# Slot loads that wait for the steady count of splits, small tables behind the second weight slot, and two activation sums behind the low parts

## The reference, cut to what matters

```python
def hybrid_layer(x, pos, ckv_past, kr_past, p):
    h = rms_norm(x, p['g_mix'])
    z = h @ p['w_in']                     # 1024 -> 256 q | 128 kv | 32 key | 512 u | 512 v
    ...                                   # latent attention (8 heads) and spatial gating
    x = x + merged @ p['w_o']             # 1024 -> 1024
    h2 = rms_norm(x, p['g_ffn'])
    x = x + (jax.nn.silu(h2 @ p['w_gate']) * (h2 @ p['w_up'])) @ p['w_down']   # 1024 -> 2816 -> 1024
    return x, c_kv, k_r, v_rows
```

## Time and profile before

| | |
|---|---|
| time, median of 3 runs | 1525.26 us (1521.08 to 1540.3) |
| the profiled execution's own time | 1518.49 us |
| its span, first to last instruction | 1516.7 us |
| mean granted TensorE clock | 0.966 |
| PE busy | 1369.4 us (90%) |
| PE weight loads busy | 1259.9 us (83%) |
| DVE busy | 902.1 us (59%) |
| POOL busy | 847.3 us (56%) |
| ACT busy | 577.0 us (38%) |
| HBM read | 98.10 MB, 67 GB/s over the span |

### The profile page before, as it was taken

One profiled execution on the slowest core, in us unless ns is written; L12 is line 12 of the kernel. 1 busy time (PEld: TensorE's weight loads), 2 busy tenths in 40 slices (PEclk: granted clock), 3 DMA queues, 4 the chain that ended last, 5 costly groups with the idle time before them and its releaser, 6 DMA issues.

```text
span 1516.7 us, 25316 instructions
## 1 busy us (share of the span) xinstructions
PE 1369.4 (90%) x9496; PEld 1259.9 (83%) x9496; DVE 902.1 (59%) x1490; ACT 577.0 (38%) x925; POOL 847.3 (56%) x452
## 2 busy tenths in 40 slices
PE   6998978978989898989879989899699898989898
PEld 6885656978989898989778755679699898989898
DVE  3458567256757575756544585762666666656575
ACT  4335566242323333333142354662333333333331
POOL 4535247436767575757264443454476666757571
PEclk9999999989999999999989999999899999999999
DMA  6200011112131313223321000011122223131321
GB/s 214 77 20 9 1 56 57 49 36 84 57 111 55 106 60 101 65 90 104 93 77 56 24 4 29 29 56 56 39 73 75 93 72 94 58 108 56 110 83 63
DMA packets 125967, 102.33 MB, mean 67 GB/s; under 512 B 8652, under 2 KB 112528, under 8 KB 125904
## 3 DMA queue, kind: packets, MB, share of 16 engines
q1 hardware_dynamic: 123240, 100.46, 21.4%
q10 hardware_dynamic: 2664, 1.02, 0.3%
HBM read 98.10 MB, written 3.36 MB: 67 GB/s over the span
## 4 chain that ended last, share of the span: by engine, by line
PE 36%; issue 23%; POOL 22%; DVE 13%; ACT 3%; DMA 2%; SPq 1%; ACTq 0%; POOLq 0%; DVEq 0%
POOL w_lo L865 8%; PE ps L2139 7%; POOL w_lo_a L865 5%; PE ps L1810 3%; PE ps L1814 3%; PE ps L1811 3%; PE ps L1793 3%; PE ps L1795 3%; PE ps L1794 3%; POOL w_lo L875 3%; PE ps L1755 3%; PE ps L2043 2%; DVE hs_lo L1246 2%; POOL gate L852 2%; PE ps L2023 2%
## 5 line engine op out<-in xcount | busy, mean ns | idle before, releaser
L735 POOL TENSOR_TENSOR rs<-ms,mhalf 128x8 f32<-128x8 f32 (+5 forms) x66 | 140.5, 2133 | 219.6 <-DVE ms L1372 82.4
L1628 DVE TENSOR_REDUCE raw<-raw 128x512 f32<-128x1024 f32 x168 | 210.6, 1255 | 54.8 <-DMA raw<-in_w_gate 54.7
L865 POOL TENSOR_TENSOR w_lo<-raw,w_hi 128x512 fp32r<-128x512 f32 (+1 forms) x120 | 201.6, 1710 | 36.6 <-ACT w_hi L1192 36.6
L865 POOL TENSOR_TENSOR w_lo_a<-raw,w_hi_a 128x512 fp32r<-128x512 f32 x80 | 161.3, 2027 | 89.7 <-ACT w_hi_a L1192 89.7
L1810 PE MATMUL ps<-act_hi,w_hi 128*128 128x288 f32 x704 | 197.1, 295 | 15.9 <-DVE xT L1587 12.3
L1811 PE MATMUL ps<-act_lo,w_hi 128*128 128x288 f32 x704 | 197.0, 295 | 0.0
L2139 PE MATMUL ps<-t_hi,w_hi 128*128 128x288 f32 x480 | 148.0, 308 | 41.8 <-DVE side L1669 41.8
L1587 DVE TENSOR_TENSOR xT<-ps,xT 128x576 f32<-128x576 f32 x192 | 142.9, 754 | 69.8 <-PE ps L1814 69.7
L728 POOL TENSOR_TENSOR w_lo<-raw,w_hi 128x2048 fp32r<-128x2048 f32 (+1 forms) x25 | 113.0, 4523 | 95.3 <-ACT w_hi L895 95.3
L1810 PE MATMUL ps<-hs_hi,w_hi 128*128 128x288 f32 x448 | 129.7, 304 | 28.5 <-DVE hs_lo L1246 28.5
L875 POOL TENSOR_TENSOR w_lo<-raw,w_hi 128x2048 fp32r<-128x2048 f32 x20 | 92.5, 4627 | 110.3 <-ACT w_hi L1211 110.3
(11 more groups left out here) (242 smaller groups left out, 3509.1 us busy)
## 6 DMA issues: line engine op xcount, KB each, us to landing
raw<-in_w_gate SPq DMA_DIRECT2D x80, 256.0 KB, 3.5
raw<-in_w_down SPq DMA_DIRECT2D x20, 1024.0 KB, 5.0
raw<-in_w_up SPq DMA_DIRECT2D x80, 256.0 KB, 3.8
raw<-in_w_in SPq DMA_DIRECT2D x10, 1024.0 KB, 5.2
raw<-in_w_o SPq DMA_DIRECT2D x8, 1024.0 KB, 5.0
x_tm<-in_x_prompt SPq DMA_DIRECT2D x4, 512.0 KB, 4.9
raw<-in_w_gate SPq DMA_DIRECT2D x2, 1024.0 KB, 5.4
raw<-in_w_up SPq DMA_DIRECT2D x2, 1024.0 KB, 6.6
```

The costliest lines, as they stand in the source:

```text
L735: pool.tensor_tensor(rs[:, c:c + n], ms[:, c:c + n], mhalf[:, 0:n], ALU.pow).then_inc(rs_ready, 1)
L865: pool.tensor_tensor(lo[:, k, cols], src, hi[:, k, cols].bitcast(F32), ALU.subtract).then_inc(lo_split, 1)
L1628: dve.tensor_reduce(raw[:, 2, j * Q:(j + 1) * Q], added(a, b), AX.X, ALU.add).then_inc(sums_added, 1)
```

## The change

The loop's slot loads wait for another count: slots.ready[n + 4] less one turn's pieces, in place of slots.ready[n - 2]. For the six slots of a turn the two are equal except for the first, n0, where the new count is lower by four; the old condition for turn 0 stands as a wait of its own ahead of the loop. The small tables of layer 1 are issued behind the load of its second input slot, with the wait for the last block's end; that slot's load itself gets a wait for the quarter sums. The third and fourth x sum come behind the low parts: the third in r_by_token between ms and the wait for the root, the fourth after r's copy; POOL's differences stand ahead of the square sum of the same tile, with a wait for that tile's addition, and ScalarE's high halves follow. r is spread along columns in the first up tile and no longer in the second gate tile; its units are the bank of ss2 (Ring.again) and one new bank, closed after both gate tiles, so that two banks less are dealt out.

```diff
--- before.py
+++ after.py
@@ -111,6 +111,13 @@
         self.values[sem] = self.values.get(sem, 0) + 1
         u = Unit(len(self.units), None, self.before(), (sem, self.values[sem]))
         self.units.append(u)
+        return u
+
+    def again(self, u, sem):
+
+        self.values[sem] = self.values.get(sem, 0) + 1
+        u = Unit(u.n, None, u.freed, (sem, self.values[sem]))
+        self.units[u.n] = u
         return u
 
     def close(self, u):
@@ -340,10 +347,11 @@
 
         def sums():
             L["ss2"] = ring.add("sumsq_out")
-            ring.skip()
-            L["rb"] = [ring.add("rb_out") for _ in range(2)]
+            L["rb"] = [ring.again(L["ss2"], "rb_out"), ring.open("rb_out")]
 
         L["g0"] = pair_units(L["ffn_in"][0], between=sums)
+        for u in L["rb"]:
+            ring.close(u)
         L["u0f"] = pair_units(L["ffn_in"][1])
         def block(n):
             b = Block(ring)
@@ -655,6 +663,8 @@
             sp.dma_start(x_tm[DEC:P, PT_, :], a["x_sample"][0]).then_inc(x_loaded[PT_], 16)
             for l, L in enumerate(plan):
                 for n, (rows, c0, c1) in zip(L["w_in"], w_in_parts):
+                    if l and n == L["w_in"][1]:
+                        sp.wait_ge(sums_added, SUMS * l)
                     load(n, by_k(n, c1 - c0, (rows.stop - rows.start) // P), in_cols(l, rows, c0, c1))
                     if l == 0 and n == L["w_in"][1]:
                         sp.wait_ge(g_zeroed, 1)
@@ -663,6 +673,9 @@
                         for t, c in enumerate(TILE_AT):
                             sp.dma_start(trig[:, t, :], a["trig"][c:c + P, :]).then_inc(trig_loaded, 16)
                         small(0)
+                    if l and n == L["w_in"][1]:
+                        sp.wait_ge(S["ffn_out"], plan[l - 1]["end_out"])
+                        small(l)
                 n = L["wq"]
                 load(n, raw[:, n % 2, 0:2 * HEADS * QK].rearrange("p (m n) -> p m n", m=2),
                      a["w_q_up"][l].rearrange("(m p) n -> p m n", p=P))
@@ -678,11 +691,12 @@
                 for n, src in zip(L["ffn_in"], (gate_src, up_src)):
                     load(n, by_k(n, COLS), src[0])
                 n0 = L["body_slots"][0]
+                sp.wait_ge(lo_split, slots.ready[n0 - 2])
                 with sp.Fori(0, BODIES) as b:
                     for s in range(2):
                         for j in range(3):
                             n = n0 + 3 * s + j
-                            sp.wait_ge(lo_split, b * L["body_pieces"] + slots.ready[n - 2])
+                            sp.wait_ge(lo_split, b * L["body_pieces"] + (slots.ready[n + 4] - L["body_pieces"]))
                             if j == 1:
                                 sp.dma_start(by_f(n), down_src[b * 2 + s]).then_inc(raw_loaded[n % 2], 16)
                                 continue
@@ -694,10 +708,6 @@
                 for q in range(4):
                     cols = slice(q % 2 * WIDTH, (q % 2 + 1) * WIDTH)
                     sp.dma_start(by_f(n)[:, q // 2, cols], down_src[FPAIRS - 1][:, q // 2, cols]).then_inc(raw_loaded[n % 2], 16)
-                if l + 1 < DEPTH:
-                    sp.wait_ge(sums_added, SUMS * (l + 1))
-                    sp.wait_ge(S["ffn_out"], L["end_out"])
-                    small(l + 1)
             for e in range(2):
                 cols = slice(e * WIDTH, (e + 1) * WIDTH)
                 for t in range(NT):
@@ -831,18 +841,19 @@
 
                     if k >= 2:
                         pool.wait_ge(t_lo_done, KT // 2 * l + k - 1)
+                    emptied(pool, L["wo"][k + KT // 2][0])
                     pool.tensor_tensor(x_sums[:, k % 2, 0, :], xT[:, k, 0:HALF], xT[:, k, HALF:TOK], ALU.subtract
                                        ).then_inc(x_differed, 1)
 
                 for j, n in enumerate(L["w_o"][2:] + L["ffn_in"][:1]):
                     for k in range(2 * j, 2 * j + 2):
-                        sum_squares(2 * l + 1, [k])
                         if k >= KT // 2:
                             difference(k - KT // 2)
+                        sum_squares(2 * l + 1, [k])
                     w_low(n)
                 for k in range(6, KT):
+                    difference(k - KT // 2)
                     sum_squares(2 * l + 1, [k])
-                    difference(k - KT // 2)
                 root(l, "r2", NT)
                 w_low(L["ffn_in"][1])
 
@@ -1142,7 +1153,7 @@
                     if k in (2, 4, 6):
                         w_high((L["w_o"][2:] + L["ffn_in"][:1])[k // 2 - 1])
                     square_output(k)
-                    if k >= KT // 2:
+                    if k in (4, 5):
                         t_high(k - KT // 2)
                 filled(act, L["wo"][-1][1])
                 for k in range(KT):
@@ -1151,7 +1162,8 @@
                     high_part(k, G_FFN + KT * l)
                 w_high(L["ffn_in"][1])
 
-                t_high(KT // 2 - 1)
+                t_high(2)
+                t_high(3)
 
                 def silu(f, sem, no):
                     act.wait_ge(sem, no)
@@ -1274,13 +1286,14 @@
                 dve.wait_ge(hs_hi_done, m * KT + k + 1)
                 low(hs_lo[:, k, :], xT[:, k, :], gT[:, gcol + k:gcol + k + 1], hs_hi[:, k, :]).then_inc(hs_lo_done, 1)
 
-            def r_by_token(l, name, u, no):
+            def r_by_token(l, name, u, no, between=lambda: None):
 
                 filled(dve, u)
                 dve.tensor_scalar(ms[:, 0:NT], bank(u, cols=NT), 1.0 / D_MODEL, EPS, ALU.mult, ALU.add
                                   ).then_inc(S["sumsq_out"], 1)
                 emptied(dve, u)
                 dve.tensor_copy(ms[:, 0:NT], ms[:, 0:NT]).then_inc(ms_ready, 1)
+                between()
                 dve.wait_ge(rs_ready, root_no(l, name))
                 dve.tensor_copy(r_tok[:, 0:NT], rs[:, 0:NT]).then_inc(r_ready, 1)
                 dve.wait_ge(r_ready, no)
@@ -1610,7 +1623,7 @@
                 for m in range(KT):
                     filled(dve, L["wo"][m][1])
                     add_to_x(m, L["wo"][m][0]).then_inc(S["wo_added"], 1)
-                    if KT // 2 <= m < KT - 1:
+                    if m in (4, 5):
                         x_sum(m - KT // 2)
                 for k in range(KT):
                     low_part(2 * l + 1, k, G_FFN + KT * l)
@@ -1628,8 +1641,8 @@
                     dve.tensor_reduce(raw[:, 2, j * Q:(j + 1) * Q], added(a, b), AX.X, ALU.add).then_inc(sums_added, 1)
 
                 n0 = L["body_slots"][0]
-                x_sum(KT // 2 - 1)
-                r_by_token(l, "r2", L["ss2"], 2 * l + 2)
+                r_by_token(l, "r2", L["ss2"], 2 * l + 2, lambda: x_sum(2))
+                x_sum(3)
                 filled(dve, L["rb"][0])
                 dve.tensor_copy(rb[:, 0:SEQ], bank(L["rb"][0])).then_inc(S["rb_out"], 1)
                 filled(dve, L["rb"][1])
@@ -2112,7 +2125,7 @@
                     for u in L["g0"][f]:
                         free(u)
                     by_feature(L["g0"][f], slots.raw[n] % 2, f * P, COLS, KT, hs_hi, hs_lo,
-                               ready=r_along_columns if f else
+                               ready=None if f else
                                lambda k: pe.wait_ge(hs_lo_done, (2 * l + 1) * KT + k + 1))
                     if f == 0:
                         pe.wait_ge(summed, (2 * l + 2) * KT)
@@ -2122,7 +2135,8 @@
                 for f in range(2):
                     for u in L["u0f"][f]:
                         free(u)
-                    by_feature(L["u0f"][f], slots.raw[n] % 2, f * P, COLS, KT, hs_hi, hs_lo)
+                    by_feature(L["u0f"][f], slots.raw[n] % 2, f * P, COLS, KT, hs_hi, hs_lo,
+                               ready=None if f else r_along_columns)
                 emptied(pe, L["rb"][1])
                 emptied(pe, L["g0"][1][1])
                 pe.wait_ge(t_lo_done, KT // 2 * (l + 1))
```

## The result

The changed kernel takes 1445.5 us (median of 4 runs) where the kernel before took 1530.3 beside it: a ratio of 0.944, 95% interval 0.936 to 0.953. The forecast was 1441, its range 1428 to 1464.

A forecast was written before the change was run, and what follows sets the result against it. TensorE's waits were taken as the bound: side copies, low halves, x. Parts of 57.2, 14.0 and 11.0, 82.2 us off the profiled 1518.49, gave 1436.3; plus 4.7, 1441 us. Range 1428 to 1464.

The forecast's parts named there:

- Part 1: FFN loop slot loads: gate load goes out 13 us earlier, all eight slow pairs become 22.31 us; -57.2 us.
- Rivals B and C: B: loop finds another wait, 28.6 us missing, 1470, chance 0.07; C: gate load goes no earlier, 57.2 missing, 1498, 0.03.
- Part 2: Layer change: first input weights load ahead of the small tables, so TensorE's wait on x goes; -14.0 us.
- Part 3: FFN start: x sums moved behind the low parts, r into the up slot; -11.0 us over two layers, bounds 0 and -17.
- the held case: FFN start: third x sum's last step is held by POOL's split of the up slot; stretch 51.6 us.
- rival A: FFN start gives nothing back, as r, broadcast, gate eviction and pieces become the wait; 11 us missing, 1452; chance 0.15.
- the free case: FFN start: third x sum runs unhindered beside POOL's split, r copied at 333.8; stretch 49 us.
- r in the up slot: FFN start: r spread in the first up tile, with two PSUM banks less, costs nothing else.
- Rival D: FFN loop without gaps: granted clock falls to half in part of it; slower, 1616 with a quarter; chance 0.03.
- the 4.7 us between the profiled execution and the median: Added to the summed 1436.3 us, between the timed runs' lowest (2.6) and median (6.8) above the profiled execution.

The follow-up runs named there:

- the fourth experiment: The changed kernel with r spread in the second gate tile again and the banks of the kernel before; 1446.5 us, ratio 0.947 to the kernel before.
- the start alone: The kernel before with only the new order of the x sums and r in the up slot; 1529.2 us, ratio 0.999.
- the reordered kernel: The changed kernel with r in the gate tile, x sums' low halves and weight sums later, POOL's up-slot split after r's copy; 1424.4 us, repeats 1445.9 (another chip), 1427.4.

## Why the prediction was right, and the term that was too large

**Part 1, right.** Forecast -57.2 us, measured -57.2, by itself and in the whole. The mechanism is the one named: the gate load goes out as the down split ends, and what follows it is what followed in the undisturbed half turns. Rivals B and C, another wait in the loop and a count that does not act, are out by the pairs.

**Part 2, right.** Forecast -14.0, measured -14.2, by itself -14.0. The chain came out as worked: POOL's split begins 1.8 us after TensorE starts the last down weights (714.59 against 712.76; forecast 2.0), and VectorE's first low part ends 7.1 us after that start (forecast 7.2).

**Part 3, the mechanism right, the term mis-sized:** "The stretch becomes 49 or 51.6 us. I take the held case" gave -11.0 us; measured 55.40 and 54.43, which is -4.4, more than half of the way to the bound of 0 that is rival A. The choice between the two cases was right, the held one came. The third x sum's last step is stretched beside the split, 4.91 us, r is copied at 339.25, and with the split ahead of the root the step took 0.51 us and the starts were 3.2 and 1.9 us shorter (forecast for the free case: 2.6 less in each). The Trainium skill, SBUF — State Buffer, "Who interferes with whom", says that a VectorE instruction with two SBUF inputs contends with a GpSimd instruction that reads SBUF, and that the one issued first keeps the port to its end; this trace and that experiment agree. The 3.8 us between 51.6 and 55.4 in layer 0 come from three terms:
- *Low parts, and what hangs on them: +1.9.* The forecast took 7.6 us for eight, as they ran before. Eight that have VectorE nearly to themselves, at the program's start, take 5.91 us (row of 17.64 above). Before, POOL worked beside the FFN's eight for 3.2 us (one square sum, one difference, 327.65 to 330.87), and 1.7 us were lost. In the changed order the end of its split, two differences and two square sums run beside them from 318.0 to 325.0, and 3.9 us are lost. This is the contention that the forecast applied to one instruction and not to these eight. The broadcast was copied at 343.86, not 341.7, of which 0.26 us is the later end of w_o. With the differences held back POOL worked beside them for 4.5 us, and 2.8 us were lost (8.72 in all). The loss thus rises with the time that POOL works beside them; 1.1 us of the 3.9 was taken away by an experiment, the rest is read from these rows.
- *From the broadcast to the third low piece: +0.9.* 16.3 us, not 15.4. POOL's two big pieces took 2.89 and 2.87 us where the earlier trace rows have 2.41, and operations of VectorE with two SBUF inputs run beside them: two multiplications from 353.36, 4.59 us for the pair, and two subtractions from 357.87, 4.65 us. This was not tested by itself.
- *The block's last part: +1.0.* From 360.21 to 372.56, 12.35 us where 9.6 + 1.7 was allowed. The granted clock is at its lower level from 355.6, behind the wait of 2.4 us and ahead of that of 3.16, until 365.8 (window 360.21:365.80 above: 23 matmuls in 5.59 us). At full clock these would take 3.1 us, so the lower clock costs 2.5 us of this part and not 1.7.

"r in the up slot" was costed at nothing. It is no gain, and by the fourth experiment perhaps 0.3 to 1.2 us of a loss.

**Rival D** does not occur: the loop's pairs have a granted clock of 1.00, in both layers.

The forecast came out 4.5 us too low: 6.6 us of part 3 and 2.9 us of the rest were missing, while the 4.7 us between the profiled execution and the median were not needed, as this profile lies at its own median. That these two errors took each other half away is luck; by its sum alone the forecast was 1436.3, 9.3 us under the profiled execution.

## What to carry to other kernels

A steady loop's prefetch wait should be written from the slot that becomes free in the steady state and not from the first turn; one load held for four splits too many cost 57 us, while two too many cost nothing, so the price has to be read from the cover and not from the count. When work moves on VectorE, look up what POOL does in the new place for each instruction with two SBUF inputs, not for the largest alone: there a chain of short operations pays several times. Copies need the same look: two of 5 elements were held until the end of POOL's split, for 4.49 us before and for 2.17 us with the split ahead of the root, where they otherwise take 0.17. And a wait of TensorE that moves to a later tile gains nothing when the same engine's queue still sets the end; here taking work off the path to the broadcast, and moving the split that held it, gained 20 us over two layers.

## What was not expected of the hardware

The same instructions of the attention run at either of TensorE's two clocks, depending on the execution. The window of that stretch in the kernel after, then in the second profiled execution of the same kernel, and in that of the kernel with the late gate load:

```profile
889.00:963.00 74.00, 61.46 (x363) 1.00 0.15 50
```

```profile
923.00:973.00 50.00, 50.00 (x173) 0.50 0.06 21
```

```profile
889.00:963.00 74.00, 64.34 (x267) 0.71 0.09 29
```

In the second the granted clock is 0.50 for some 50 us on end, while TensorE is busy all the time; the waits before it (2.26 us at 914.5, 1.49 us at 920.5) are the same as in the first, which kept 1.00. The last w_o matmul of layer 1 ends at 1045.15 and not at 1025.42, 19.7 us later, which is all that the two spans differ by. Such stretches of 17 to 31 us also stood in the profiles of the start alone, the split before the root, the kernel with the differences held back and the first two of the reordered kernel, and never in the FFN loop. They come at few places. In layer 1 three begin 199.8 to 200.1 us after the kv projection and two 181 to 183 us after it; the three of layer 0 begin at 232.3 to 233.0. All begin in the attention's products, 0.1 to 2.6 us after the end of a wait of TensorE of 0.9 to 1.5 us that the executions without the stretch have too. The price is read from executions of one kernel: between the kv projection and the last w_o matmul of layer 1 the reordered kernel takes 283.95 us without a stretch and 297.8 with one of 30.7.

They explain the differences between the profiled executions of one kernel, and in the six runs of the kernel after that were made beside the reordered one the time goes with the clock: 0.983 to 0.988 as a mean in the three of 1443.5 to 1446.3 us, 0.967 to 0.974 in the three of 1460.1 to 1465.3. They are why a window of the place that was changed told more than a median of four. What decides between the clocks wasn't found.
